# Output projection as three products of rounded parts in a one-layer attention and mixture-of-experts kernel

## The reference, cut to what matters

```python
hx = modulate(x, norm_g[i, 0], sh1, sc1)
...
mx = neighbourhood_attention(q, k, v, kc, vc, na_rpb[a]) @ na_w_o[a]
x = x + g1 * rms_norm(mx, norm_g[i, 1])
hx2 = modulate(x, norm_g[i, 2], sh2, sc2)
...
for e in range(N_EXPERTS):
    hid = xt @ w_up[e] + b_up[e]
    x_glu = jnp.minimum(hid[:, :D_EXPERT], SWIGLU_LIMIT)
    x_lin = jnp.clip(hid[:, D_EXPERT:], -SWIGLU_LIMIT, SWIGLU_LIMIT)
    act = x_glu * jax.nn.sigmoid(SWIGLU_ALPHA * x_glu) * (x_lin + 1)
    y = act @ w_down[e] + b_down[e]
    out = out + gates[:, e:e + 1] * y.astype(jnp.float32)
```

## Time and profile before

| | |
|---|---|
| timed runs | 1268.31, 1269.69, 1271.27 us; median 1269.69 |
| profiled execution, its time | 1267.97 us |
| its span, first to last instruction | 1266.2 us |
| PE busy | 1175.2 us, 93% |
| DVE, ACT, POOL busy | 33%, 15%, 5% |
| bytes read from HBM | 453 MB, 359 GB/s over the span |

### The profile page before, as it was taken

How to read it: one execution, slowest core, us unless ns; L and a number is a source line. 1 busy time by engine, 2 the same in 40 slices (tenths; PEclk the granted TensorE clock), 3 DMA queues, 4 the chain that set the end, 5 groups by cost and what they waited for, 6 DMA issues and landing times.

```text
span 1266.2 us, 15412 instructions
## 1 busy us (share of the span) xinstructions
PE 1175.2 (93%) x5853; PEld 503.9 (40%) x5854; DVE 418.4 (33%) x805; ACT 192.4 (15%) x397; POOL 60.1 (5%) x89
## 2 busy tenths in 40 slices
PE   5899999989999999999999999899999999999996
PEld 1888655433333333333333333333333333333332
DVE  2944364643222232222222222222222232222224
ACT  2200265111111111111111111111111111111111
POOL 2230043000000000000000000000000000000000
PEclk9999999989999999999999999999999999999998
DMA  9973487346599999999999999999699999999791
GB/s 376 378 210 134 143 266 312 120 191 267 239 430 428 428 429 430 428 428 428 430 428 427 429 431 426 429 429 430 264 430 431 428 429 427 430 429 429 308 386 45
DMA packets 49380, 454.41 MB, mean 359 GB/s; under 512 B 16792, under 2 KB 16856, under 8 KB 20656
## 3 DMA queue, kind: packets, MB, share of 16 engines
q1 hardware_dynamic: 48352, 450.90, 86.1%
q10 hardware_dynamic: 496, 1.52, 0.4%
q0 software_dynamic: 512, 1.72, 0.4%
HBM read 453.07 MB, written 1.05 MB: 359 GB/s over the span
## 4 chain that ended last, share of the span: by engine, by line
PE 51%; DMA 40%; DVE 4%; issue 2%; ACT 1%; SPq 0%; POOL 0%; DVEq 0%; ACTq 0%
DMA ring<-in_moe_w_up 38%; PE pair L1290 21%; PE pair L1360 9%; PE pair L1087 8%; PE pair L1172 2%; DMA ring<-in_ada_w 2%; PE pair L1103 1%; PE pair L1045 1%; PE pair L1113 1%; PE pair L1276 1%; PE pair L1126 1%; DVE v_mem L975 1%; DVE v_mem L967 1%; DVE v_mem L972 1%; ACT v_mem L620 1%
## 5 line engine op out<-in xcount | busy, mean ns | idle before, releaser
L1290 PE MATMUL pair<-ring,v_mem 128*64 128x512 f32 x2240 | 511.2, 598 | 43.2 <-DMA ring<-in_moe_w_up 43.1
L1290 PEld LDWEIGHTS pair<-ring,v_mem 128*64 128x64 f32 x2240 | 154.0, 136 | 325.8 <-issue 251.4
L1360 PE MATMUL pair<-ring,v_mem 128*64 128x512 f32 x1120 | 248.1, 594 | 1.4
L955 DVE TENSOR_TENSOR hT_mem<-hT_mem,pair 128x512 f32<-128x512 f32 x140 | 89.9, 684 | 213.1 <-PE pair L1279 213.1
L1360 PEld LDWEIGHTS pair<-ring,v_mem 128*64 128x64 f32 x1120 | 92.7, 137 | 132.6 <-issue 120.7
L981 DVE SCALAR_TENSOR_TENSOR hT_low<-pair,gate_slot,v_round 128x512 fp32r<-128x512 f32 x35 | 26.3, 751 | 266.6 <-ACT v_round L630 266.6
L618 ACT ACTIVATE v_mem<-pair 128x256 f32<-128x256 f32 x35 | 13.4, 383 | 457.0 <-PE pair L1334 457.0
L1216 PE MATMUL pair<-q_mem,pT_mem 128*64 128x512 f32 x288 | 69.7, 605 | 0.9 <-DVE pT_mem L895 0.9
L630 ACT ACTIVATE v_round<-pair,gate_slot 128x512 fp32r<-128x512 f32 x35 | 24.0, 687 | 231.4 <-PE pair L1360 231.4
L392 POOL TENSOR_TENSOR rstd<-ms,neghalf 128x1 f32<-128x1 f32 (+1 forms) x8 | 5.6, 706 | 1046.9 <-DVE ms L666 1046.9
L965 DVE TENSOR_SCALAR v_round<-v_mem 128x256 fp32r<-128x256 f32 x35 | 10.3, 295 | 119.3 <-ACT v_mem L618 119.2
(11 more groups left out here) (227 smaller groups left out, 1026.5 us busy)
## 6 DMA issues: line engine op xcount, KB each, us to landing
ring<-in_moe_w_up SPq DMA_DIRECT2D x128, 2048.0 KB, 25.5
ring<-in_moe_w_down SPq DMA_DIRECT2D x64, 2048.0 KB, 23.5
ring<-in_ada_w SPq DMA_DIRECT2D x24, 1024.0 KB, 9.2
ring<-in_na_w_qkv SPq DMA_DIRECT2D x12, 1024.0 KB, 27.3
ring<-in_na_w_o SPq DMA_DIRECT2D x4, 1024.0 KB, 13.9
tokens<-in_na_rpb SPq DMA_DIRECT2D x32, 96.0 KB, 6.4
gain<-in_norm_g POOLq DMA_DIRECT2D x3, 512.0 KB, 5.6
tokens<-in_x SPq DMA_DIRECT2D x1, 1024.0 KB, 5.1
```

The lines of the kernel that those rows point to most:

```text
L955: d.tensor_tensor(dst, dst, bank[banks[n]][:, :], ALU.add).then_inc(acc_done, 1)
L1290: last = mm(bank[half][64 * n:64 * n + 64, :], xT[:, k % 4, 64 * (k // 4):64 * (k // 4) + 64], w[:, c0:c0 + HALF], start=is_first and k == ...
L1360: last = mm(bank[2][64 * n:64 * n + 64, :], aT[:, j, 64 * half:64 * half + 64], w[:, HALF * n:HALF * n + HALF], start=k == 0, stop=k == KC ...
```

## The change

1. The output projection becomes three `fp32r` matmuls for each float32 one: high x low, high x high, low x high, 96 in all.
2. The weights' high parts are written by ACT (`take_wo_high(k)`, a copy of 128x1024) to ring slots 8 to 11. They stand in ACT's program at the end of duos 11 to 15 (k = 0 to 4) and behind the last copy L529 (k = 5 to 7).
3. The low parts are written by DVE (`take_wo_low(k)`, a subtraction of 128x1024) over the weights. They stand at the end of DVE's duos 12 to 15 (k = 0 to 3), before the last `take_o` (k = 4) and behind it (k = 5 to 7).
4. `take_o` does three operations in place of one: a rounding copy of 128x256, then, behind a wait for it, two subtractions of 128x128.
5. Loads j = 2 and 3 of expert 0, whose slots now hold the high parts, wait for `ring_free` 40 (the end of the output projection) in place of 34 and 36; j = 4, which waited for 38, waits for 40 too.
6. The split of `b_up` (six operations on 32x2048) moves from the output projection to behind `tables_ready`, ahead of DVE's first `block_step`. PE's wait for it moves from ahead of the first block to ahead of its `add_bias`.

```diff
-        oT = hT_mem[:, 0:2048].rearrange("p (k t) -> p k t", k=KC)
+        oT_high = hT_low_mem[:, 0:2048].rearrange("p (k t) -> p k t", k=KC)
...
+        q_round = also("q_round", [P, KC * TOK])
...
+        oT_low = [m[:, 0:1024].rearrange("p (k t) -> p k t", k=KC) for m in (q_round, pT_high)]
...
             for j in range(PER):
-                sp.wait_ge(ring_free, EXP - RING + 2 * j + 2)
+                sp.wait_ge(ring_free, EXP - RING + 2 * j + 2 if j < 2 else EXP)
                 load_expert(0, j)
...
+            def take_wo_high(k):
...
+                if k % 2 == 0:
+                    chunk_here(sc, WO + k // 2)
+                sc.wait_ge(ring_free, ADA2 + KC)
+                cols = slice(D * (k % 2), D * (k % 2) + D)
+                s.activation(ring_low[:, WO_HIGH + k // 2, cols], wpair(WO, k), ACT.Copy).then_inc(wo_high, 1)
...
                 if m >= 1:
                     take_probsT(m - 1)
+                if m > ADA2_AT:
+                    take_wo_high(m - ADA2_AT - 1)
             take_probsT(DUOS - 1)
+            for k in range(DUOS - ADA2_AT - 1, KC):
+                take_wo_high(k)
...
                 ve.wait_ge(o_done, 2 * p + 2)
-                d.tensor_copy(by_row(oT[:, p, :]), backwards(bank[6][:, 0:TOK])).then_inc(o_ready, 1)
+                step(d.tensor_copy(by_row(oT_high[:, p, :]), backwards(bank[6][:, 0:TOK])))
+                for t in range(2):
+                    toks = slice(P * t, P * t + P)
+                    ins = d.tensor_tensor(by_row(oT_low[t][:, p, :]), backwards(bank[6][:, toks]),
+                                          by_row(oT_high[:, p, toks]), ALU.subtract)
+                ins.then_inc(o_ready, 1)
+
+            def take_wo_low(k):
+
+                ve.wait_ge(wo_high, k + 1)
+                cols = slice(D * (k % 2), D * (k % 2) + D)
+                d.tensor_tensor(ring_low[:, (WO + k // 2) % RING, cols], wpair(WO, k),
+                                ring_low[:, WO_HIGH + k // 2, cols], ALU.subtract).then_inc(wo_split, 1)
...
+                if m >= ADA2_AT + 2:
+                    take_wo_low(m - ADA2_AT - 2)
             invert(DUOS - 1)
             take_o(HEADS // 2 - 2)
+            take_wo_low(DUOS - ADA2_AT - 2)
             take_o(HEADS // 2 - 1)
+            for k in range(DUOS - ADA2_AT - 1, KC):
+                take_wo_low(k)
...
-            ve.wait_ge(in_bup, 16)
-            step(d.tensor_copy(bup_parts[0:E, :], bup))
-            step(d.tensor_tensor(bup, bup, bup_parts[0:E, :], ALU.subtract))
-            step(d.tensor_copy(bup_part, bup))
-            step(d.tensor_tensor(bup, bup, bup_part, ALU.subtract))
-            d.tensor_copy(bup_parts[E:2 * E, :], bup_part)
-            d.tensor_copy(bup_parts[2 * E:3 * E, :], bup).then_inc(bup_split, 1)
...
             ve.wait_ge(tables_ready, 1)
+            ve.wait_ge(in_bup, 16)
+            step(d.tensor_copy(bup_parts[0:E, :], bup))
...
+            d.tensor_copy(bup_parts[2 * E:3 * E, :], bup).then_inc(bup_split, 1)
+            ve.wait_ge(bup_split, 2)
...
-                        if t == 0 and i == 0 and k % 2 == 0:
-                            chunk_here(pe, WO + k // 2)
+                        if t == 0 and i == 0:
+                            pe.wait_ge(wo_split, k + 1)
...
-                        last = mm(bank[4 + 2 * t + i][:, :], oT[:, k, P * t:P * t + P],
-                                  wpair(WO, k)[:, HALF * i:HALF * i + HALF], start=k == 0, stop=k == KC - 1)
+                        mm(dst, o_high_k, w_low_k, start=k == 0, stop=False)
+                        mm(dst, o_high_k, w_high_k, start=False, stop=False)
+                        last = mm(dst, o_low_k, w_high_k, start=False, stop=k == KC - 1)
...
                     start_sums(1)
+                    pe.wait_ge(bup_split, 2)
...
-            pe.wait_ge(bup_split, 1)
             block_step(0, 0, is_first=True)
```

More of the change, by code:

```diff
@@ L196, in build @@
         o_done, o_ready = sem("o_done"), sem("o_ready")
+        wo_high, wo_split = sem("wo_high"), sem("wo_split")
         wo_done, x1_ready, h2_ready = sem("wo_done"), sem("x1_ready"), sem("h2_ready")
@@ L261, in wpair @@
             return ring[:, (n + i // 2) % RING, D * (i % 2):D * (i % 2) + D]
+        WO_HIGH = 8
         def load_bias(eng, h):
@@ L945, in _ @@
             ve.wait_ge(tables_ready, 1)
+            ve.wait_ge(in_bup, 16)
+            step(d.tensor_copy(bup_parts[0:E, :], bup))
+            step(d.tensor_tensor(bup, bup, bup_parts[0:E, :], ALU.subtract))
+            step(d.tensor_copy(bup_part, bup))
+            step(d.tensor_tensor(bup, bup, bup_part, ALU.subtract))
+            d.tensor_copy(bup_parts[E:2 * E, :], bup_part).then_inc(bup_split, 1)
+            d.tensor_copy(bup_parts[2 * E:3 * E, :], bup).then_inc(bup_split, 1)
+            ve.wait_ge(bup_split, 2)
             def add_part(t, b, is_first=False, banks=(6, 7)):
@@ L1167, in _ @@
                     for k in range(KC):
-                        if t == 0 and i == 0 and k % 2 == 0:
-                            chunk_here(pe, WO + k // 2)
+                        if t == 0 and i == 0:
+                            pe.wait_ge(wo_split, k + 1)
                         if t == 1 and i == 1 and k == 0:
                             pe.wait_ge(wr_ready, 1)
-                        last = mm(bank[4 + 2 * t + i][:, :], oT[:, k, P * t:P * t + P],
-                                  wpair(WO, k)[:, HALF * i:HALF * i + HALF], start=k == 0, stop=k == KC - 1)
+                        cols = slice(D * (k % 2) + HALF * i, D * (k % 2) + HALF * i + HALF)
+                        w_high_k = ring_low[:, WO_HIGH + k // 2, cols]
+                        w_low_k = ring_low[:, (WO + k // 2) % RING, cols]
+                        o_high_k, o_low_k = oT_high[:, k, P * t:P * t + P], oT_low[t][:, k, :]
+                        dst = bank[4 + 2 * t + i][:, :]
+                        mm(dst, o_high_k, w_low_k, start=k == 0, stop=False)
+                        mm(dst, o_high_k, w_high_k, start=False, stop=False)
+                        last = mm(dst, o_low_k, w_high_k, start=False, stop=k == KC - 1)
                         if t == 1 and i == 1 and k % 2 == 1:
```

## The result

| | before | after |
|---|---|---|
| median of 7 runs | 1269.23 us (1267.63 to 1271.27) | 1274.81 us (1273.97 to 1277.82) |
| profiled execution, its span | 1266.2 us | 1272.9 us |
| mean granted clock of the span | 0.992 | 0.988 |

The ratio is 1.0052, with a 95% interval of 1.0043 to 1.0061: the change makes the kernel 5.5 to 7.7 us slower. The time is inside the range of the prediction, but the likeliest case was "no difference that can be measured", with +2.0 us, and that case did not happen.

What follows compares the result with a forecast made beforehand. The chain was taken as about half PE and 40% DMA, with PE work before 328.04 us shifting the weight stream one for one. Terms -5.92 + 5.49 + 2.42 = +2.0 us gave 1271.7 us, range 1267.3 to 1275.3.

Steps and rivals of the forecast that it cites:

- the likeliest case: Whole kernel: +2.0 us, too small to tell from no change; this case alone has 1269.5 to 1273.5 us.
- The projection: Output projection on PE: 96 `fp32r` matmuls at 0.2267 us take 21.76 us against 27.68, 5.92 less.
- Its start: Last duos ahead of the output projection: DVE becomes the bound and the projection starts 5.5 us late.
- the layout: Last duos: operations laid end to end by their waits in program order; last L789 at 221.12, projection from 227.31.
- Beside the projection: DVE and SP work during the projection: token half 0 ends near 248, reordered loads stay hidden, cover about 1 us.
- The first block: First expert block: PE's `start_sums(1)` waits for DVE behind the moved bias split, 2.4 us late.
- The weight stream: Loads from expert 2 on, from 328.04 us: start and end move one for one with the chain ahead, 2 us later.
- The step that failed: Duos and first block: PE is busy enough around its pauses, an argument against another half-clock stretch of up to 2.5 us.
- clock: Rival, pauses in duos or first block: another 1.2 GHz stretch, up to 2.5 us, 1274.2; 26% together with more contention.
- More contention: Rival, duos: each low part takes 2.20 us beside POOL, 1273.6; 26% together with the clock rival.
- The duos absorb the split: Rival, last duos: DVE's chain stays under PE's 3.11 us, projection starts at most 2 us late, 1266.2; 12%.
- Late expert chunks: Rival, reordered expert loads: they arrive late for PE, which needs them 15 us later than reckoned; 2%.

Runs made afterwards that it cites:

- the repeat: The changed kernel with no edit, profiled and timed again beside later experiments: 1275.50 us, ratio 1.0051 to the kernel before.
- the bias split in halves: Changed kernel with the first two bias-split operations moved to DVE's wait for `gain`, the other four left behind the tables: 1270.16 us, ratio 1.0011 to before.
- the one SBUF input: Kernel with the bias split in halves, its four low parts in the duos subtracting an unused PSUM bank: 1269.05 us, ratio 1.0006 to before.

## Why the prediction was right and wrong, step by step

**The projection** (-5.92): measured 22.05 against 21.76, -5.63. The starts are 0.227 apart as in the v projection (between the two rows lie 65 starts, so 66 steps, and the 0.2267 holds). Right. The sum by the pace of the Trainium skill ("TensorE: Matmul & The Clock Gate", on the 56 ns gap), 20.71, would have been 1.3 too low.

**Its start** (5.49 late): 6.44 in the trace, 7.3 in the repeat, and 5.44 once added matmuls keep the clock up. That DVE becomes the bound was right. That 5.44 lies so near 5.49 is luck: two errors cancel. DVE's low parts are not slowed (1.25 us, where 1.74 to 1.98 were counted), so in the kernel with matmuls in the pauses the last L807 starts 20.2 us behind T9, where the layout had 21.3 (221.12 - 199.83). POOL is slowed, by 1.04 us a pair, and POOL stands on the same path, between L807 and the transposes: from that L807 to the projection it is 7.2 us, where the layout had 6.2 (227.31 - 221.12). Of the 2.0 us of overlap in the sum, 0.55 us showed in the kernel that took it away. The three operations of `take_o` take 0.92 us from the first start to the last end, as the 0.91 that was taken. DVE's wait for ACT's high part, 0.67 in the layout, is 1.72 in the trace:

```profile
210.26 0.40 DVE L812 CAST hT_low<-pair 128x256 fp32r<-128x256 f32 x1
210.69 0.29 DVE L815 TENSOR_TENSOR q_round<-pair,hT_low 128x128 fp32r<-128x128 f32 x1
...
216.01 1.23 DVE L823 TENSOR_TENSOR ring_low<-ring,ring_low 128x1024 fp32r<-128x1024 f32 x1 [1.72 <-ACT ring_low L553]
```

**Beside the projection** (nothing): right, and as close as it was said to be. Token half 0 ended at 248.4 ("near 248"):

```profile
247.14 1.28 DVE L911 SCALAR_TENSOR_TENSOR q_mem<-q_mem,rstd,mod 128x1024 f32<-128x1024 f32 x1 [0.68 <-POOL rstd L397]
```

The kernel with the split back in its old place shows what the cover was worth: the stretch behind it is 2.0 us longer when it is gone.

**The first block** (+2.42): the wait is 2.47, by the operation named and at the place named. The stretch is +5.63; of the 3.16 us beyond the wait, 2.86 go when matmuls fill the pause.

**The weight stream** (one for one): right. From SP's issue for expert 2 on, both spans are equal within 0.4 us.

**The step that failed** is the one that kept the clock out of the sum. It read: "Against: every duo keeps PE busy for about 3.1 of its 4 us or so, and around the pause of the first block it is busy without a break." Both halves were read from rows that stand, and neither protects. The duos' idle time isn't spread evenly: the wait for `take_o` falls on every second duo, 1.67 us the first time and 3.08 us the second, when DVE itself had stood 1.72 us waiting for ACT. And the block's pause was enough although PE was busy on both sides of it. The clock then costs 1.0 to 1.9 us in the duos (28.25 and 29.12 against 27.25), and in the first block 1.4 us (before with the bias move, with and without added matmuls) to 2.9 us (the changed kernel with and without). In both places the cost goes with how long the half clock lasts: 3.4 us of it cost 1.0 and 1.4, 6.8 us of it 1.9 and 2.9. The sum had nothing for either. The prediction priced one such stretch at "up to 2.5 us" and gave it, together with contention, 26%. Two came. In the profiled execution the forecast's +2.0 becomes the +5.95 of the trace by 0.95 more in the duos and 3.2 more in the first block, 0.3 more in the projection, and 0.5 less in the norm and router, where the half clock of the earlier trace rows now falls otherwise (a mean of 0.66 over 261 to 266 us, where it was 0.50).

The rivals: *clock* is what happened, twice. *More contention* did not: removing it gives half a us. *The duos absorb the split* did not: 6.44 and not 2. *Late expert chunks* did not: no wait of PE names them.

Open remains why the timed cost (+5.6 in medians, +6.6 by the ratio) and the sum of the parts by themselves don't close exactly. The bias move alone costs 6.1 us timed and 4.30 in its trace from T9 to SP's issue; the bias split in halves with the changed duos 1.4 us timed and 0.07 in its trace. A trace is one execution, and the half-clock stretches differ from one to the next. The traces also differ outside the stretches compared: T9 by 3.3 us, and the rest behind SP's issue for expert 2 by 1.4 (937.8 to 939.2). So the parts' costs are known to 1 or 2 us, not better. Left open too is what decides it between the pauses seen. Those of 2.5 us in the block and of 2.8 to 3.1 us in the duos were followed by half clock each time. One of 1.7 us in the duos was followed by full clock in five traces (the changed kernel, its repeat, both places of the bias split, the one SBUF input) and by half clock in a sixth, the one with matmuls in the block's pause. So the length of the pause alone does not decide it.

## What to carry to other kernels

A wait that opens on an otherwise busy TensorE must be priced twice: its own length, and the half clock that may follow. Here 2.5 us of wait brought 1.4 to 2.9 us of clock each time, and a wait of 1.7 us brought a half-clock stretch once in six traces. When work has to be made ready for the tensor engine by a slower one, first change the order in which TensorE consumes it, so that each piece carries more work (here six matmuls for each low part and not three); that was worth 3.2 us, while moving all low parts behind the duos mostly moved the bill (4.97 us gained, 4.36 paid). And a long chain of small operations that is in the way in two places may fit in two halves.

## What the runs showed of the hardware that was not expected

- POOL's pair of one-input operations took 2.40 us in place of 1.36 beside DVE's subtraction with two SBUF inputs, which was hardly slowed itself (1.25 against 1.22). In the kernel before, it was DVE whose operation stretched (2.20 us) beside a two-input operation of POOL (1.61 us). Who pays isn't fixed. There DVE's operation had started 0.49 us after POOL's and ended 1.08 us after it: the later one waited. In the changed kernel POOL's second operation and DVE's subtraction start within 0.01 us of each other, at 211.10, and POOL's takes 1.73 us, where one alone takes 0.69.
- The granted clock fell to 0.50 behind a single pause of 2.47 us, with PE busy ahead of it and behind it, in all three traces with this pause unfilled (the changed kernel twice, the bias move alone); in the two where float32 matmuls without use filled it, it stayed at 1.00.
- The same pause cost different amounts: the block was 65.99 us with the bias move alone and 67.47 in the changed kernel. The half clock behind it lasted 3.4 us in the one and 6.8 in the other. The window from 286 to 292, at 0.50 in the changed kernel, is with the bias move alone:

```profile
286.00:292.00 6.00, 6.00 (x24) 1.91 (x23) 2.37 (x5) 2.39 (x4) 0.00 (x0) 0.72 0.76 325
```
